# A two-layer decoder trunk on one core: the loop over the layers written out in the code, and the last residual update of a layer interleaved with the split for the next layer's first products

## The chip, the cores and the metric

The kernel runs on one core of one Trainium2 chip. The metric is the device time of one execution in microseconds (us). An execution holds the whole inference step, both layers and all stored states.

## What is computed

The reference is a trunk of two equal layers over 336 tokens (8 running sequences of 8 new tokens, 16 meta tokens, a prompt of 256). In short, with `L` the layer:

```python
for l in range(DEPTH):                                   # DEPTH = 2
    f = swiglu(rmsnorm(x, ln_ffn1_pre[l]), ffn1_w_in[l], ffn1_w_out[l])
    x = x + 0.5 * rmsnorm(f, ln_ffn1_post[l])
    m, s, c, p = mixer(rmsnorm(x, ln_mix_pre[l]), ssm[l], conv[l], pool[l], ...)
    x = x + rmsnorm(m, ln_mix_post[l])
    f = swiglu(rmsnorm(x, ln_ffn2_pre[l]), ffn2_w_in[l], ffn2_w_out[l])
    x = x + 0.5 * rmsnorm(f, ln_ffn2_post[l])
```

The mixer projects `x`, runs a causal convolution of width 4 over 24 tiles of 128 channels, a chunked state-space scan (SSD) over 32 heads, a pooling branch with windows of 2 to 16 tokens, and merges both through sigmoid gates. Everything is float32.

## The kernel before

**Layout.** Activations stand channel-major: `x` is 8 tiles (KD) of 128 channels by 336 tokens. A product with float32 weights is made of three matmuls per 128x128 weight tile. Both operands are split into a high part and the remainder: `gb += whi*ahi + whi*alo + wlo*ahi`. Weights come in units of 8 tiles (512 KB). SyncE loads a unit into one of four slots of `wraw`, ScalarE (ACT) makes `whi` (L430), GpSimd (POOL) makes `wlo` (L355), TensorE (PE) uses both.

**Activations.** For the norm ahead of a product ACT makes `ahi` of each `x` tile and its square (`split_x`, L452, L455), GpSimd adds the squares (L377, L381), and VectorE (DVE) makes `alo` (`split_tile`, L691). The products run on the unnormalised split. Their results are multiplied by the inverse root mean square `rpre` (L681), which arrives later.

**Joins.** I call a join the stretch in which `x` is updated and split for the next products. There are three kinds per layer: after the first feed-forward block (into the mixer), after the mixer (into the second feed-forward block), and between the layers. `update_x` does for each tile `t_a = fo*gain*rms` (L699), `x += t_a` (L701) and a drain (L704). At the first two joins it is called with `nxt`, so that the split of tile `s - 2` stands between the updates. At the join of the layers it is called without. The splits stand at the head of the next pass of the loop over `L`. PE takes the split tiles in `first_units` (L1065 to L1069), four units side by side, so that it can start at the first split tile.

**Mixer.** After its join come 8 convolution tiles (B and C of the scan) and the first of 16 x tiles, as straight code in the body of the layer loop. `conv` multiplies by the first tap (L744) and adds three more (L747), each with a drain ahead. Then come 16 SSD steps. Twelve stand in a hardware loop over `g` with four steps in its body, and the last four are written out behind it. A step on DVE makes, in the order of the code: the convolution of tile t+1, chained states (L787, L792), the masked product (L768), `t_a` (L810, L812, L814, L817), the new states (L825, L826) and the split `blo` (L830). The two operands of L814 and L817 and the weight units of the step hang on the other engines.

Of the kernel before, what the change touches and what calls it, by code (L numbers as in the profile page):

```python
# [23 lines left out]
D_MODEL, D_FF, D_INNER, DEPTH = 1024, 2816, 2048, 2  # L24
# [5 lines left out]
KD, KF, KI = D_MODEL // P, D_FF // P, D_INNER // P  # L30
# [90 lines left out]
def slot_of(phase, n):  # L121

    return (U0[phase] + n) % RING
# [25 lines left out]
def build(nc, x_in, wts, par_in, con_in, own_dram, cst_in, pst_in, ssm_in, y_out, ssm_out, conv_out, pool_out):  # L149
    with ExitStack() as ctx:  # L150
# [177 lines left out]
        @block.sync  # L328
        def _(sp_):
            def unit(u, slot):  # L330
                sp_.wait_ge(w_rawfree, u + 1)
                sp_.dma_start(wraw[:, slot, :], wts[u, :, :]).then_inc(w_landed[slot], 16)

            def units(L, u0, u1):
                with sp_.Fori(u0 // RING, u1 // RING) as i:
                    for s in range(RING):
                        unit(L * UNITS + RING * i + s, s)

            with sp_.Fori(0, DEPTH) as L:
                units(L, 0, U0["f1o"])  # L340
                sp_.wait_ge(s_hfree, L + 1)
                sp_.dma_start(cst[:, :, :], cst_in[L, :, :, :]).then_inc(s_hist, 16)
                units(L, U0["f1o"], UNITS)
            for s in range(AHEAD):
                sp_.wait_ge(w_rawfree, DEPTH * UNITS + s + 1)
                sp_.dma_start(wraw[:, s, :], wts[s, :, :]).then_inc(w_landed[s], 16)

        @block.gpsimd
        def _(pool):  # L350
            pool.sem_inc(w_rawfree, RING)

            def lo(u, s):
                pool.wait_ge(w_hi, u + 1)
                pool.tensor_tensor(wlo[:, s, :], wraw[:, s, :], whi[:, s, :].bitcast(F32), ALU.subtract).then_inc(w_lo, 1)  # L355
                pool.wait_ge(w_lo, u + 1)
                pool.sem_inc(w_rawfree, 1)

            def ahead(L, u):
                lo(L * UNITS + u + AHEAD, (u + AHEAD) % RING)  # L360

            def run(L, u0, u1):

                n = (u1 - u0) // RING
                with pool.Fori(0, n) as i:
                    for s in range(RING):
                        lo(L * UNITS + u0 + AHEAD + RING * i + s, (u0 + AHEAD + s) % RING)
                for u in range(u0 + n * RING, u1):
                    ahead(L, u)

            def sum_x(L, u, n, s0):

                ahead(L, u)
                for k in range(1, KD):
                    pool.wait_ge(sq_done, L * N_SQ + s0 + k + 1)
                    if k == 1:
                        pool.tensor_tensor(acc[:, :], sq[:, 0, :], sq[:, 1, :], ALU.add).then_inc(x_sum, 1)  # L377
                        ahead(L, u + 1)
                    else:
                        pool.wait_ge(x_sum, L * N_XSUM + n * (KD - 1) + k - 1)  # L380
                        pool.tensor_tensor(acc[:, :], acc[:, :], sq[:, k % RING, :], ALU.add).then_inc(x_sum, 1)  # L381

            def ssd_step(L, t, q, last):

                u = U0["ssd"] + 2 * t
                if not last:
                    lo(L * UNITS + u + 1 + AHEAD, slot_of("ssd", 2 * q + 1 + AHEAD))
                pool.wait_ge(dec_done, L + 1)
                pool.wait_ge(st_landed, 16 * (L * KI + t) + 16)
                pool.wait_ge(so_free, 16 * (L * KI + t) + 16)  # L390
                ds_ = dec[:, 2 * DK:].rearrange("p (b h) -> p b h", b=SEQS)[:, :, bass.ds(2 * t, 2)]
                pool.tensor_tensor(so[:, 0:SEQS * P].rearrange("p (b h d) -> p b h d", b=SEQS, h=2),
                                   st[:, :].rearrange("p (b h d) -> p b h d", b=SEQS, h=2), rep(ds_, HEAD_DIM, 3), ALU.mult).then_inc(st_dec, 1)
                lo(L * UNITS + U0["ssd"] + z_at(t, last) + AHEAD, slot_of("ssd", z_at(q + 2, last) + AHEAD))

            for s in range(AHEAD):
                lo(s, s)
            pool.wait_ge(s_con, 32)
            pool.tensor_copy(maskr[:, :], own_in[:, 0:2 * P])
            pool.tensor_copy(identr[:, :], cc(C_ID))  # L400
            pool.tensor_copy(halfr[:, :], own_in[0:HEAD_DIM, 2 * P:4 * P]).then_inc(consts, 1)
            with pool.Fori(0, DEPTH) as L:
                sum_x(L, 0, 0, 0)
                run(L, 2, U0["dt"])
                sum_x(L, U0["dt"], 1, S_X1)
                run(L, U0["dt"] + 2, U0["ssd"] + 1)
                with pool.Fori(0, N_GROUPS - 1) as g:
                    for j in range(TILES_PER_GROUP):
                        ssd_step(L, TILES_PER_GROUP * g + j, j % 2, False)
                for j in range(TILES_PER_GROUP):  # L410
                    ssd_step(L, KI - TILES_PER_GROUP + j, j % 2, j == TILES_PER_GROUP - 1)
                run(L, U0["mix"], U0["f2i"])
                sum_x(L, U0["f2i"], 2, S_X2)
                run(L, U0["f2i"] + 2, UNITS)
# [3 lines left out]
        def _(act):  # L418
# [133 lines left out]
            act.dma_start(con[:, :], con_in).then_inc(s_con, 16)  # L552
            act.dma_start(own_in, own_dram).then_inc(s_con, 16)
            act.wait_ge(s_eps, 1)
            with act.Fori(0, DEPTH) as L:
                split_x(L, G_F1A, 0, 0, "f1i")
                root(L, ST_F1A)
                ffn_in(L, "f1i", V_F1)
# [96 lines left out]
        def _(dve):  # L655
# [32 lines left out]
            def split_tile(L, k, gain, h0):  # L688

                dve.wait_ge(hi_done, L * N_HI + h0 + k + 1)  # L690
                dve.scalar_tensor_tensor(alo[:, k, :], x[:, k, :], pcol(L, gain + k), ahi[:, k, :].bitcast(F32),  # L691
                                         ALU.mult, ALU.subtract).then_inc(a_done, 1)

            def update_x(L, gain, nxt=None):

                lag = 2
                for s in range(KD + (lag if nxt else 1)):
                    if s < KD:
                        dve.scalar_tensor_tensor(t_a[:, s % RING, :], fo[:, s, :], pcol(L, gain + s), kb[0][:, 0:T], ALU.mult, ALU.mult)  # L699
                    if 1 <= s <= KD:  # L700
                        dve.tensor_tensor(x[:, s - 1, :], x[:, s - 1, :], t_a[:, (s - 1) % RING, :], ALU.add).then_inc(val_in, 1)  # L701
                    if nxt and s >= lag:
                        split_tile(L, s - lag, *nxt)
                    dve.drain()  # L704

            def ffn_in(L, ph_, h0, gt0):
# [124 lines left out]
                                         ALU.mult, ALU.subtract).then_inc(b_done, 1)  # L831
                dve.drain()  # L832

            with dve.Fori(0, DEPTH) as L:

                for k in range(KD):
                    split_tile(L, k, G_F1A, 0)
                inverse(L, ST_F1A, rpre)
                ffn_in(L, "f1i", H_F1, 0)
                out_tiles(L, "f1o", S_F1)  # L840
# [155 lines left out]
                ffn_in(L, "f2i", H_F2, KF + KI + 2 * KD)  # L996
                out_tiles(L, "f2o", S_F2)
                inverse(L, ST_F2B)
                update_x(L, G_F2B)

        @block.tensor
        def _(pe):
# [161 lines left out]
                    pe.wait_ge(y_read, kt + 1)  # L1165
                    x_token_major(L, t + 1, 1 - q)

            with pe.Fori(0, DEPTH) as L:
                ffn(L, "f1", 0, 0, 0, ST_F1A, ST_F1B)

                first_units(L, "dt", KD, 1, ST_MA)
# [230 lines left out]
```

## Time and profile before

| what | before |
|---|---|
| time, median of 3 runs | 2289.95 us (2285.34 to 2296.04) |
| profiled execution: span from first to last instruction | 2279.0 us |
| profiled execution: own time | not recorded beside its span; the median of the runs is 10.95 us above the span |
| PE busy | 2087.2 us, 92% |
| DVE busy | 1095.6 us, 48% |
| ACT busy | 937.1 us, 41% |
| POOL busy | 1248.3 us, 55% |
| chain that ended last | PE 64%, DVE 17%, DVEq 10%, issue 5% |

### The profile page before, as it was taken

Reading aid. Unit: us, or ns where it says so; the run is one execution under the profiler, and the core shown is the slowest. Engines: PE = TensorE matmul, PEld = TensorE weight load, DVE = VectorE, ACT = ScalarE, POOL = GpSimd, SP = SyncE. Lnnn points to the kernel's source line nnn. Section 1 sums busy time; section 2 is a strip of 40 time slices with the busy share of each in tenths; the row PEclk is TensorE's granted clock in tenths of the full one; section 3 lists DMA queues with packets and bytes.
Section 4 is the critical chain, followed back from the end, with each engine's and each line's share of the span. In section 5 each row is a group of like instructions: output and inputs, shape, how many; then the busy total and the mean of one; then the engine's idle time right before and its main releaser. Section 6 shows DMA issues by size and latency. Waiting matters only on the chain.

```text
span 2279.0 us, 40931 instructions
## 1 busy us (share of the span) xinstructions
PE 2087.2 (92%) x13546; PEld 2026.9 (89%) x13546; DVE 1095.6 (48%) x2040; ACT 937.1 (41%) x1357; POOL 1248.3 (55%) x555
## 2 busy tenths in 40 slices
PE   6999878999989998999889998699998999989997
PEld 6999877888889997999879998688888999979997
DVE  3221277888944525221242213778888445252212
ACT  4343344444533434333343333444444334343432
POOL 5666642333356665666656676333333566656675
PEclk9999998999999999999999999889999999999998
DMA  4445422333344443444424453223333444434443
GB/s 172 138 144 157 138 67 84 128 118 121 116 150 139 139 143 97 146 139 148 141 91 141 147 156 115 76 97 115 115 115 128 146 139 142 144 99 141 138 156 108
DMA packets 86338, 292.38 MB, mean 128 GB/s; under 512 B 15728, under 2 KB 15728, under 8 KB 86256
## 3 DMA queue, kind: packets, MB, share of 16 engines
q1 hardware_dynamic: 68544, 249.13, 34.6%
q10 hardware_dynamic: 17712, 42.22, 5.3%
q8 instruction: 44, 0.72, 0.1%
q14 instruction: 38, 0.31, 0.0%
HBM read 269.29 MB, written 22.02 MB: 128 GB/s over the span
## 4 chain that ended last, share of the span: by engine, by line
PE 64%; DVE 17%; DVEq 10%; issue 5%; POOL 1%; ACT 1%; DMA 1%; ACTq 0%; POOLq 0%; SPq 0%
PE gb L1013 20%; PE gb L1017 19%; PE gb L1016 19%; DVE cv L747 6%; DVEq L746 2%; DVE t_a L814 2%; DVEq L704 2%; DVEq L832 1%; POOL wlo L355 1%; DVE alo L691 1%; DVEq L777 1%; DVEq L811 1%; PE gb L1065 1%; DVE t_a L699 1%; DVE t_a L812 1%
## 5 line engine op out<-in xcount | busy, mean ns | idle before, releaser
L355 POOL TENSOR_TENSOR wlo<-wraw,whi 128x1024 fp32r<-128x1024 f32 x474 | 1141.7, 2409 | 952.3 <-ACT whi L430 933.2
L1013 PE MATMUL gb<-ahi,whi 128*128 128x336 f32 x2256 | 750.6, 333 | 23.9 <-POOL wlo L355 14.6
L1017 PE MATMUL gb<-ahi,wlo 128*128 128x336 f32 x2256 | 722.5, 320 | 0.0
L1016 PE MATMUL gb<-alo,whi 128*128 128x336 f32 x2256 | 721.9, 320 | 0.0
L430 ACT ACTIVATE whi<-wraw 128x1024 fp32r<-128x1024 f32 x474 | 494.1, 1050 | 188.9 <-PE gb L1013 116.5
L1013 PEld LDWEIGHTS gb<-ahi,whi 128*128 128x128 f32 x2256 | 433.3, 192 | 36.0 <-POOL wlo L355 27.3
L1016 PEld LDWEIGHTS gb<-alo,whi 128*128 128x128 f32 x2256 | 433.3, 192 | 0.0
L1017 PEld LDWEIGHTS gb<-ahi,wlo 128*128 128x128 f32 x2256 | 430.6, 191 | 0.0
L1013 PE MATMUL gb<-bhi,whi 128*128 128x336 f32 x1248 | 395.4, 317 | 5.0 <-DVE blo L967 5.0
L1016 PE MATMUL gb<-blo,whi 128*128 128x336 f32 x1248 | 393.4, 315 | 0.0
L1017 PE MATMUL gb<-bhi,wlo 128*128 128x336 f32 x1248 | 393.1, 315 | 0.0
L713 DVE TENSOR_TENSOR t_a<-gb,rpre 128x336 f32<-128x336 f32 x176 | 88.6, 507 | 337.9 <-PE gb L1017 336.3
L1013 PEld LDWEIGHTS gb<-bhi,whi 128*128 128x128 f32 x1248 | 234.8, 188 | 5.6 <-issue 5.6
L1016 PEld LDWEIGHTS gb<-blo,whi 128*128 128x128 f32 x1248 | 235.3, 189 | 0.0
L1017 PEld LDWEIGHTS gb<-bhi,wlo 128*128 128x128 f32 x1248 | 235.0, 188 | 0.0
L726 DVE COPY fo<-gb 128x336 f32 x48 | 24.4, 508 | 294.0 <-PE gb L1017 294.0
L747 DVE SCALAR_TENSOR_TENSOR cv<-xp,par,cv 128x360 f32<-128x360 f32 x144 | 147.3, 1023 | 29.5 <-issue 29.5
L474 ACT ACTIVATE bhi<-t_b 128x336 f32 (+1 forms) x88 | 42.7, 485 | 249.8 <-DVE t_b L716 249.8
L1065 PE MATMUL gb<-ahi,whi 128*128 128x336 f32 x192 | 68.3, 356 | 52.2 <-DVE alo L691 49.8
L487 ACT ACTIVATE sq<-fo 128x336 f32 x48 | 23.3, 486 | 224.9 <-DVE fo L726 224.9
L495 ACT ACT_TABLE_LOAD x38 | 48.8, 1283 | 136.4 <-DVE cv L747 135.8
L470 ACT ACTIVATE t_b<-t_a 128x336 f32<-128x336 f32 x88 | 42.7, 486 | 119.7 <-DVE t_a L713 119.7
(166 smaller groups left out, 2316.7 us busy)
## 6 DMA issues: line engine op xcount, KB each, us to landing
wraw<-wts SPq DMA_DIRECT2D x474, 512.0 KB, 3.5
ssm_o<-tail ACTq DMA_DIRECT2D x32, 576.0 KB, 3.7
st<-ssm_in ACTq DMA_DIRECT2D x32, 512.0 KB, 4.4
x<-x_in ACTq DMA_DIRECT2D x2, 672.0 KB, 5.0
y<-x ACTq DMA_DIRECT2D x2, 672.0 KB, 3.0
pool_o<-tail ACTq DMA_DIRECT2D x2, 540.0 KB, 4.9
tail<-pst_in ACTq DMA_DIRECT2D x2, 480.0 KB, 4.3
conv_o<-cso ACTq DMA_DIRECT2D x48, 13.5 KB, 3.4
```

What stands on the lines that cost most here:

```text
L355: pool.tensor_tensor(wlo[:, s, :], wraw[:, s, :], whi[:, s, :].bitcast(F32), ALU.subtract).then_inc(w_lo, 1)
L430: act.activation(whi[:, slot, :], wraw[:, slot, :], ACT.Copy).then_inc(w_hi, 1)
L495: act.activation(seqs(dst[:, 0:SAMPLE], STEPS), seqs(cv[:, 0:CP], CSTRIDE)[:, :, 0:STEPS], ACT.Silu, bias=bias)
L704: dve.drain()
L713: dve.tensor_tensor(t_a[:, r, :], gb[r][:, 0:T], rpre[:, :], ALU.mult).then_inc(g_out, 1)
L746: dve.drain()
L747: ins = dve.scalar_tensor_tensor(cv[:, :], xp[:, k:k + n], pcol(L, G_CW + CONV_K * c + k), cv[:, :], ALU.mult, ALU.add)
L814: dve.scalar_tensor_tensor(t_a[:, 2, :], xs[:, q, :], pcol(L, G_D + t), t_a[:, 1, :], ALU.mult, ALU.add)
L1013: ins = pe.matmul(gb[bank][:, 0:T], whi[:, slot, w], xh, start=first and j == 0, stop=False)
L1016: pe.matmul(gb[bank][:, 0:T], whi[:, slot, w], xl, start=False, stop=False)
L1017: ins = pe.matmul(gb[bank][:, 0:T], wlo[:, slot, w], xh, start=False, stop=last and j == tiles - 1)
L1065: ins = pe.matmul(gb[s][:, 0:T], whi[:, s, w], ahi[:, j, :], start=j == 0, stop=False)
```

## The change

The hardware loop over the layers becomes a loop of the program that writes the code: on all five engines both layers are written out, and `L` is a constant. The inner hardware loops stay. `update_x` gets an argument `ahead`, and at the end of layer 0 it is called with the split for layer 1's first products. The splits at the head of a layer remain for layer 0 alone.

```diff
-            with sp_.Fori(0, DEPTH) as L:
+            for L in range(DEPTH):
...
-            with act.Fori(0, DEPTH) as L:
+            for L in range(DEPTH):
...
-            def update_x(L, gain, nxt=None):
+            def update_x(L, gain, nxt=None, ahead=0):
...
                     if nxt and s >= lag:
-                        split_tile(L, s - lag, *nxt)
+                        split_tile(L + ahead, s - lag, *nxt)
                     dve.drain()
...
-            with dve.Fori(0, DEPTH) as L:
-
-                for k in range(KD):
-                    split_tile(L, k, G_F1A, 0)
+            for L in range(DEPTH):
+
+                if L == 0:
+                    for k in range(KD):
+                        split_tile(L, k, G_F1A, 0)
...
-                update_x(L, G_F2B)
+                update_x(L, G_F2B, (G_F1A, 0) if L + 1 < DEPTH else None, 1)
```

(GpSimd and TensorE get the same line in place of their `Fori` over `L`.)

```order
L699 ISA
L699 SCALAR_TENSOR_TENSOR t_a<-fo,par,kb 128x336
L701 TENSOR_TENSOR x<-x,t_a 128x336
L699 ISA
L699 SCALAR_TENSOR_TENSOR t_a<-fo,par,kb 128x336
L701 TENSOR_TENSOR x<-x,t_a 128x336 x2
L834 REGISTER_ALU
L834 COMPARE_AND_BRANCH
```

The head of the loop's body, to which that branch goes:

```order
L834 ISA
L691 ISA
L691 SCALAR_TENSOR_TENSOR alo<-x,par,ahi 128x336
L690 REGISTER_ALU
L691 ISA
L691 SCALAR_TENSOR_TENSOR alo<-x,par,ahi 128x336
```

The same place in the changed kernel, from the first updates on:

```order
L699 SCALAR_TENSOR_TENSOR t_a<-fo,par,kb 128x336 x2
L701 TENSOR_TENSOR x<-x,t_a 128x336
L699 SCALAR_TENSOR_TENSOR t_a<-fo,par,kb 128x336
L701 TENSOR_TENSOR x<-x,t_a 128x336
L691 SCALAR_TENSOR_TENSOR alo<-x,par,ahi 128x336
L699 SCALAR_TENSOR_TENSOR t_a<-fo,par,kb 128x336
L701 TENSOR_TENSOR x<-x,t_a 128x336
L691 SCALAR_TENSOR_TENSOR alo<-x,par,ahi 128x336
```

The eight splits moved up between the updates, as at the other joins. The branch and all register operations of this place are gone.

**Place two: DVE in a step of the SSD loop**, the middle of `ssd_step`. Before, the registers `L` and `g` both enter the sums:

```order
L805 ISA
L806 TENSOR_TENSOR t_b<-gb,rpre 128x336
L810 TENSOR_TENSOR t_a<-kb,eab 128x336
L812 TENSOR_TENSOR t_a<-kb,t_a 128x336
L814 ISA
L814 SCALAR_TENSOR_TENSOR t_a<-t_b,par,t_a 128x336
L816 ISA
L817 TENSOR_TENSOR t_a<-t_a,t_b 128x336
```

In the changed kernel:

```order
L805 REGISTER_ALU
L806 TENSOR_TENSOR t_b<-gb,rpre 128x336
L810 TENSOR_TENSOR t_a<-kb,eab 128x336
L812 TENSOR_TENSOR t_a<-kb,t_a 128x336
L814 ISA
L814 SCALAR_TENSOR_TENSOR t_a<-t_b,par,t_a 128x336
L816 REGISTER_ALU
L817 TENSOR_TENSOR t_a<-t_a,t_b 128x336
```

Operations and their order are the same. Two groups of register operations became single ones, and the group at L814 is left with `g` alone to reckon with.

**Place three: DVE in a convolution of the straight code ahead of the SSD steps.** Before:

```order
L744 ISA
L744 TENSOR_SCALAR cv<-xp,par 128x360
L747 ISA
L747 SCALAR_TENSOR_TENSOR cv<-xp,par,cv 128x360
L747 ISA
L747 SCALAR_TENSOR_TENSOR cv<-xp,par,cv 128x360
```

In the changed kernel these rows are the tensor operations alone:

```order
L744 TENSOR_SCALAR cv<-xp,par 128x360
L747 SCALAR_TENSOR_TENSOR cv<-xp,par,cv 128x360 x3
```

The register operations of all straight code left the stream. The same holds for the four SSD steps that stand behind the loop over `g`.

## Rows read from the trace of the kernel before

**Rows 1.** The page: span, busy time of the engines, instruction fetches, chain by engine.

```profile
span 2279.0 us, 40931 instructions
PE 2087.2 (92%) x13546; PEld 2026.9 (89%) x13546; DVE 1095.6 (48%) x2040; ACT 937.1 (41%) x1357; POOL 1248.3 (55%) x555
q14 instruction: 38, 0.31, 0.0%
PE 64%; DVE 17%; DVEq 10%; issue 5%; POOL 1%; ACT 1%; DMA 1%; ACTq 0%; POOLq 0%; SPq 0%
```

**Rows 2.** Windows: length, busy PE, PEld, DVE, ACT, POOL, then PEclk, DMA share, GB/s.

```profile
378.00:597.00 219.00, 201.93 (x1397) 184.89 (x1395) 189.67 (x348) 106.66 (x173) 79.94 (x36) 0.97 0.37 122
...
897.00:1043.00 146.00, 144.90 (x938) 144.62 (x938) 44.08 (x83) 58.07 (x81) 93.40 (x40) 1.00 0.45 144
...
1132.00:1166.00 34.00, 18.29 (x109) 17.61 (x108) 18.30 (x26) 14.92 (x24) 13.96 (x10) 0.73 0.11 33
```

**Rows 3.** Timeline of DVE: first update and `rpre` of four joins.

```profile
272.14 0.56 DVE L699 SCALAR_TENSOR_TENSOR t_a<-fo,par,kb 128x336 f32<-128x336 f32 x1 [1.86 <-PE kb L1043]
296.91 0.51 DVE L681 COPY rpre<-kb 128x336 f32<-128x336 f32 x1 [4.94 <-PE kb L1043]
...
870.23 0.56 DVE L699 SCALAR_TENSOR_TENSOR t_a<-fo,par,kb 128x336 f32<-128x336 f32 x1 [1.14 <-PE kb L1043]
895.21 0.51 DVE L681 COPY rpre<-kb 128x336 f32<-128x336 f32 x1 [4.95 <-PE kb L1043]
...
1132.36 0.56 DVE L699 SCALAR_TENSOR_TENSOR t_a<-fo,par,kb 128x336 f32<-128x336 f32 x1 [1.86 <-PE kb L1043]
1165.80 0.51 DVE L681 COPY rpre<-kb 128x336 f32<-128x336 f32 x1 [4.95 <-PE kb L1043]
...
2004.51 0.56 DVE L699 SCALAR_TENSOR_TENSOR t_a<-fo,par,kb 128x336 f32<-128x336 f32 x1 [1.27 <-PE kb L1043]
2029.81 0.51 DVE L681 COPY rpre<-kb 128x336 f32<-128x336 f32 x1 [4.94 <-PE kb L1043]
```

**Rows 4.** Timelines of DVE, PE and ACT at the join of the layers.

```profile
1146.70 1.04 DVE L691 SCALAR_TENSOR_TENSOR alo<-x,par,ahi 128x336 fp32r<-128x336 f32 x2 [3.31 <-issue]
...
1147.50 0.64 PE L1065 MATMUL gb<-ahi,whi 128*128 128x336 f32 x1 [15.29 <-DVE alo L691]
...
1148.18 1.06 ACT L430 ACTIVATE whi<-wraw 128x1024 fp32r<-128x1024 f32 x1 [11.18 <-PE gb L1065]
```

**Rows 5.** Timeline of DVE: L812 in SSD steps 4, 6, 12 and 14.

```profile
447.20 0.51 DVE L812 TENSOR_TENSOR t_a<-kb,t_a 128x336 f32<-128x336 f32 x1
...
482.09 0.51 DVE L812 TENSOR_TENSOR t_a<-kb,t_a 128x336 f32<-128x336 f32 x1
...
590.96 0.51 DVE L812 TENSOR_TENSOR t_a<-kb,t_a 128x336 f32<-128x336 f32 x1
...
624.90 0.51 DVE L812 TENSOR_TENSOR t_a<-kb,t_a 128x336 f32<-128x336 f32 x1
```

**Rows 6.** Chain that ended last: start, us, what; one loop step, one written-out step.

```profile
477.24 0.13 DVEq L747
477.42 0.59 DVE cv L747
478.08 0.13 DVEq L747
...
603.77 0.06 DVEq L747
603.83 0.05 issue
603.88 0.59 DVE cv L747
```

**Rows 7.** Timelines of DVE, ACT and POOL in SSD step 5.

```profile
457.25 2.09 DVE L747 SCALAR_TENSOR_TENSOR cv<-xp,par,cv 128x360 f32<-128x360 f32 x1 [0.24 <-issue]
...
457.03 1.92 POOL L392 TENSOR_TENSOR tail<-st,dec 128x1024 f32<-128x1024 f32 x1 [0.44 <-POOL wlo L355]
```

**Rows 8.** Timeline of DVE in the straight code of the mixer.

```profile
317.07 0.59 DVE L747 SCALAR_TENSOR_TENSOR cv<-xp,par,cv 128x360 f32<-128x360 f32 x1 [0.17 <-issue]
...
317.87 0.26 DVE L872 TENSOR_TENSOR sq<-sq 128x96 f32<-128x96 f32 x1
318.20 0.26 DVE L874 TENSOR_TENSOR sq<-sq 128x96 f32<-128x96 f32 x1
```

More of the change, by code:

```diff
@@ L401, in _ @@
             pool.tensor_copy(halfr[:, :], own_in[0:HEAD_DIM, 2 * P:4 * P]).then_inc(consts, 1)
-            with pool.Fori(0, DEPTH) as L:
+            for L in range(DEPTH):
                 sum_x(L, 0, 0, 0)
@@ L832, in ssd_step @@
                 dve.drain()
-            with dve.Fori(0, DEPTH) as L:
-                for k in range(KD):
-                    split_tile(L, k, G_F1A, 0)
+            for L in range(DEPTH):
+                if L == 0:
+                    for k in range(KD):
+                        split_tile(L, k, G_F1A, 0)
                 inverse(L, ST_F1A, rpre)
@@ L1166, in ssd_step @@
                     x_token_major(L, t + 1, 1 - q)
-            with pe.Fori(0, DEPTH) as L:
+            for L in range(DEPTH):
                 ffn(L, "f1", 0, 0, 0, ST_F1A, ST_F1B)
```

## The prediction

> **What bounds the kernel now.** I read the page first. PE is busy for 92% of the span, but the chain that ended last runs through PE for only 64% of it and through DVE and its sequencer for 27% [rows 1]. So there are stretches in which PE isn't the limit. The windows say which. In the feed-forward stretch from 897 to 1043 us PE is busy for 144.9 of 146 us, so nothing that another engine saves there is worth anything. In the 12-step SSD stretch of layer 0, 378 to 597 us, PE has 201.9 of 219 us and DVE 189.7. At the join of the layers, 1132 to 1166 us, PE has 18.3 of 34 us and a mean clock of 0.73 of full speed [rows 2]. The change acts on the two last kinds of stretch, in two ways that I price apart: the splits that move (one place), and the register `L` that becomes a constant (all places).
>
> **The moved splits.** I measure a join from the start of the first update to the start of the copy into `rpre`. Three joins already interleave: 272.14 to 296.91 is 24.77 us, 870.23 to 895.21 is 24.98 us, 2004.51 to 2029.81 is 25.30 us. The join of the layers takes 1165.80 - 1132.36 = 33.44 us [rows 3]. What it does too much is seen in its parts. The first split starts at 1146.70, behind all updates and 3.31 us of idle time that no engine caused: the branch back to the head of the loop. PE waited 15.29 us for that split. ACT, which had stopped after two tiles because it must make a weight tile whose slot PE frees with its first matmul, waited 11.18 us for PE [rows 4]. After the change the DVE stream at this place is that of the other joins, and so are the streams of ACT, POOL and PE, which already were in that order. The new wait on the way is that a split stands ahead of the next update on DVE and waits for ACT's `ahi`. Behind it in the queue stand the next update and, through it, ACT and PE. The three joins contain this wait, so I need no price for it. The gain is 33.44 - 25.02 (their mean) = 8.4 us, with bounds of 8.1 and 8.7 us from the three. SyncE, which loads weights four units ahead, and POOL, whose next `wlo` comes earlier here, have room: the DMA share in this window is 0.11 [rows 2].
>
> **The constant, in the SSD loop.** The operations don't change, their cover does. A register operation costs only where DVE stands idle for it, right behind a drain. In a loop step the fused group at each L747 stands in the chain with 0.13 us. In the four steps that are written out behind the loop, where only `L` is left in the sum, it takes 0.06 us [rows 6]. These four steps are the experiment I need, since a loop step of the changed kernel has only `g` left. From step 4 to step 6 there are 482.09 - 447.20 = 34.89 us, from step 12 to step 14, which stand at the same places of a group of four, 624.90 - 590.96 = 33.94 us [rows 5]. That is 0.475 us a step. Three groups at L747 explain 3 x 0.07 = 0.21 us of it; the rest I put on other groups like them (L733, L814, L816), on ACT and POOL. There are 24 loop steps in the two layers: 24 x 0.475 = 11.4 us. The bounds are nothing and 24 x 0.6 = 14 us.
>
> **The constant, in straight code.** Here the whole operation goes. At L747 DVE is idle for 0.17 us; between two drained operations without a register, 317.87 + 0.26 to 318.20, for 0.07 us [rows 8]. So 0.10 us is saved at each such place. There are 18 convolutions ahead of the loops (9 a layer) and 8 SSD steps behind them with three such places each, 0.30 us. One of the three lies ahead of a stall behind POOL (next part) and I don't count it: 26 x 0.20 = 5.2 us, between 0 and 8 us. In the updates of the joins each of the 8 tiles has one such place. Half of them I take to be hidden by ACT or POOL: 5 joins x 8 x 0.10 / 2 = 2.0 us, between 0 and 4. For the scalars of dt, the pooling start and the ends of the product stages I add 1.0 us, between 0 and 3.
>
> **Code.** The written-out streams are about twice as long, but each engine still runs the same number of instructions in a straight line, and the inner loops stay as they are. I take it to cost nothing. The cover is that instruction transfers run while the engines work: they are 38 packets of 0.31 MB in one queue [rows 1]. What it costs without cover is a rival below.
>
> **Sum.** 8.4 + 11.4 + 5.2 + 2.0 + 1.0 = 28.0 us. The span of 2279.0 becomes 2251.0 us. The median of the runs lies 10.95 us above the span, so I expect 2289.95 - 28.0 = 2262 us, 1.2% less.
>
> **Rivals.**
>
> *Only the join counts (0.07).* GpSimd stalls DVE: the first L747 of step 5 took 2.09 us where an undisturbed one takes 0.59, and ended with GpSimd's product of 1.92 us that began at 457.03 [rows 6, 7]. What DVE saves ahead of such a stall is lost, unless the GpSimd operation moves with it. If these stalls take all savings of registers, 8.4 us are left: 2281.5 us, within 0.5% of before. Against it: the written-out steps have the same stalls and are shorter all the same [rows 5]. The Trainium skill (SBUF — State Buffer, Who interferes with whom) says that the port pair shared by GpSimd and VectorE is an exclusive lock held for a whole instruction, not a split of bandwidth. By that rule each saving ahead of a stall is worth nothing and each behind it is worth all; the 2.09 us of this case agrees.
>
> *PE becomes the limit of the SSD steps (0.08).* PE is busy for 201.9 of 219 us [rows 2], which leaves 17.1 us for about 12 steps, 1.4 us a step. The 0.475 us fit in that, but PE must sit right: if its idle time is needed elsewhere in the step, half of 11.4 and half of 5.2 are lost and the time is 2270 us. Still faster.
>
> *Slower: the loops miss their code (0.03).* The branch back over a whole layer cost DVE 3.31 us of idle time [rows 4]. If an inner loop now lay so that each of its branches back paid that, the price would be 3.31 us an iteration. From the code, DVE takes 28 inner branches back in a layer (two feed-forward inputs of 10, three output loops of 1, the SSD loop 2, the pooling branch 3), 56 in all. It takes (28.0 + 11.4) / 3.31 = 12 of them on the path to make the kernel slower by 0.5%. The SSD loops have 4 and their bodies are the longest, so they alone would only eat 13 us. Against it: no inner branch back shows such a stall now, and nothing but the place of the bodies changes. The Trainium skill (Runtime: NRT & Kernel Launch, Instruction fetch mechanics) says that code is fetched ahead in a straight line, and that a taken branch to a block that isn't held costs a fetch. It calls full unrolling the way around. The 3.31 us of this case agree. By that page, where a body lies against the blocks decides, and the change moves all of them: that is this rival, and no row here can exclude it.
>
> **How the numbers follow.** Forecast 0.82, with its own range of 2250 to 2272 us; the three rivals 0.07, 0.08, 0.03. The low end of my range is all upper bounds, 8.7 + 14 + 8 + 4 + 3 = 38 us, or 2252 us, with 3 us for the spread of the runs, whose extremes lie 0.3% from their median. The high end takes in the case in which PE limits, the lower halves of the terms of registers, and that spread, up to 2278 us. About 0.5% (11.5 us) is what a measurement of this kernel can tell from no change. Faster by more than that: 0.82 of the forecast, nearly all, with 0.08 of the second rival, 0.90. Within: 0.07. Slower: 0.03.
>
> **What would show it.** In the profile of the changed kernel the join of the layers takes 24 to 25.5 us, PE's longest wait there is below 5 us, and the 3.31 us idle time is gone. SSD steps of the loop have the period of the old written-out ones: 33.9 us from the L812 of step 4 to that of step 6, where it was 34.89. The chain shows DVEq L747 with 0.06 in the loop and not at all in straight code, where the idle time ahead of L747 is 0.07 us. If the join shrank and the steps didn't, the first rival is right. If steps shrank and PE's waits in them went, it is the second. Idle time of some 3 us behind inner branches would be the third. A PE clock that falls at other places than now would move some us either way.

## The result, and the profile of the changed kernel

The changed kernel takes 2253.17 us (median of 4 runs, 2248.9 to 2254.58), beside 2287.64 us for the kernel before (2283.06 to 2296.04). The ratio is 0.9831 with a 95% interval of 0.9805 to 0.9857. The runs made beside the experiments give more: the kernel before has a median of 2290.7 us over 79 of them, and the changed one, its first four included, 2254.1 us over 13. So the change saves 36.6 us, 1.6%. I had forecast 28 us, 1.2%. The direction and most of the places are right, the size is a quarter too small.

The page of the changed kernel, the lines that answer to [rows 1], and the group of L747:

```profile
span 2252.3 us, 39690 instructions
...
PE 2086.7 (93%) x13546; PEld 2028.8 (90%) x13546; DVE 1095.7 (49%) x2040; ACT 931.0 (41%) x1354; POOL 1249.5 (55%) x555
...
q14 instruction: 30, 0.25, 0.0%
...
PE 70%; DVE 16%; DVEq 8%; issue 3%; ACT 1%; POOL 1%; DMA 1%; ACTq 0%; SPq 0%
...
L747 DVE SCALAR_TENSOR_TENSOR cv<-xp,par,cv 128x360 f32<-128x360 f32 x144 | 140.3, 975 | 17.8 <-issue 12.4
```

The work is the same: PE has 2086.7 us as before, DVE 1095.7, and ACT alone is 6 us shorter. L747 had 29.5 us of idle time ahead of it before and has 17.8 now. What went is time between operations: PE now holds 70% of the chain where it held 64%.

The join of the layers, timeline of DVE (start, us, what, idle ahead), against [rows 3, 4]:

```profile
1124.32 1.20 DVE L699 SCALAR_TENSOR_TENSOR t_a<-fo,par,kb 128x336 f32<-128x336 f32 x2 [1.74 <-PE kb L1044]
...
1127.10 0.56 DVE L691 SCALAR_TENSOR_TENSOR alo<-x,par,ahi 128x336 fp32r<-128x336 f32 x1
...
1148.49 0.51 DVE L681 COPY rpre<-kb 128x336 f32<-128x336 f32 x1 [4.95 <-PE kb L1044]
```

The first split starts 2.8 us behind the first update (14.3 us before), and the join takes 1148.49 - 1124.32 = 24.17 us instead of 33.44. PE's waits in this stretch are short, where the longest was 15.29 us:

```profile
PE gb L1066 <- DVE alo L691: 4.1, 2, 3.4
```

Its windows row answers to the third of [rows 2]: a PEclk of 0.81 where it was 0.73.

```profile
1122.50:1150.00 27.50, 21.15 (x115) 19.89 (x116) 17.70 (x29) 13.15 (x23) 15.27 (x11) 0.81 0.12 39
```

Two convolutions on the timeline of DVE, in the straight code and in loop step 6, against [rows 7, 8]:

```profile
315.22 1.93 DVE L747 SCALAR_TENSOR_TENSOR cv<-xp,par,cv 128x360 f32<-128x360 f32 x3
...
471.92 2.14 DVE L747 SCALAR_TENSOR_TENSOR cv<-xp,par,cv 128x360 f32<-128x360 f32 x1 [0.18 <-issue]
474.24 0.59 DVE L747 SCALAR_TENSOR_TENSOR cv<-xp,par,cv 128x360 f32<-128x360 f32 x1 [0.17 <-issue]
```

In straight code the three stand in one row with nothing between them but the drain: (1.93 - 3 x 0.59) / 2 = 0.08 us. In the loop the idle time ahead of each is 0.17 us where it was 0.24. The first of step 6 still stalls behind GpSimd, 2.14 us (2.08 us before). In step 5, where [rows 7] has 2.09 us, it now takes 0.59 us: the stall met another operation. The steps 4 and 6 of layer 0 on the timeline of DVE, against [rows 5]; they are 35.05 us apart:

```profile
443.88 0.51 DVE L812 TENSOR_TENSOR t_a<-kb,t_a 128x336 f32<-128x336 f32 x1
...
478.93 0.51 DVE L812 TENSOR_TENSOR t_a<-kb,t_a 128x336 f32<-128x336 f32 x1
```

The chain through a loop step (start, us, what), against [rows 6]:

```profile
1532.47 0.07 DVEq L747
1532.54 0.05 issue
1532.59 0.59 DVE cv L747
```

All the fused groups of this line, by its own view:

```profile
L747 DVEq FUSED_REGOPS  x72: 57/61/65, 364.8 to 1675.1; - x72
```

They were 144 of 57 to 135 ns. Half are gone, the rest cost 0.06 us.

**Where the time went.** Three profiles of each kernel (first ones, and those of experiments e0, e15, e11, e12), cut at the same DVE instructions, both layers together; mean us, and the difference:

| stretch | before | after | difference | forecast |
|---|---|---|---|---|
| join of the layers | 33.5 | 24.2 | -9.4 | -8.4 |
| mixer's straight part, `rpre` to the first loop convolution | 137.4 | 131.4 | -6.0 | -3.6 |
| SSD, step 0 to 12 | 435.0 | 429.4 | -5.6 | -11.4 |
| SSD, step 12 to the copy into `rpost` | 140.1 | 134.6 | -5.5 | -1.6 |
| `rpost` to the join | 423.7 | 420.7 | -3.0 | -1.0 |
| the four other joins | 100.5 | 99.5 | -1.0 | -2.0 |
| all else | 1015.8 | 1015.4 | -0.4 | 0 |
| span | 2285.9 | 2255.2 | -30.8 | -28.0 |

### The profile page after: what moved, and what is told of

It reads as the page before. It is cut to its first block, busy times and chain, and to the rows that moved or that the text cites. A ratio compares the mean times of both kernels' runs of the same rounds, so it can differ in the third digit from the quotient of the medians.

```text
span 2252.3 us, 39690 instructions
## 1 busy us (share of the span) xinstructions
PE 2086.7 (93%) x13546; PEld 2028.8 (90%) x13546; DVE 1095.7 (49%) x2040; ACT 931.0 (41%) x1354; POOL 1249.5 (55%) x555
## 3 DMA queue, kind: packets, MB, share of 16 engines
q1 hardware_dynamic: 68544, 249.13, 33.5%
## 4 chain that ended last, share of the span: by engine, by line
PE 70%; DVE 16%; DVEq 8%; issue 3%; ACT 1%; POOL 1%; DMA 1%; ACTq 0%; SPq 0%
PE gb L1014 21%; PE gb L1017 20%; PE gb L1018 20%; DVE cv L747 5%; DVEq L746 2%; DVE t_a L814 2%; PE gb L1066 1%; PE gb L1069 1%; PE gb L1070 1%; DVEq L704 1%; DVEq L832 1%; DVEq L811 1%; DVE t_a L699 1%; POOL wlo L355 1%; DVE xp L736 1%
## 5 line engine op out<-in xcount | busy, mean ns | idle before, releaser
L747 DVE SCALAR_TENSOR_TENSOR cv<-xp,par,cv 128x360 f32<-128x360 f32 x144 | 140.3, 975 | 17.8 <-issue 12.4
L1148 PEld LDWEIGHTS kb<-bc,st 128*128 128x128 f32 x512 | 90.3, 194 | 0.0
```

The costliest lines, as they stand in the source:

```text
L747: ins = dve.scalar_tensor_tensor(cv[:, :], xp[:, k:k + n], pcol(L, G_CW + CONV_K * c + k), cv[:, :], ALU.mult, ALU.add)
L1148: pe.matmul(kb[1][:, c], st[:, b * P:(b + 1) * P], bc[:, cg, c], start=True, stop=True)
```

## The experiments

**The scatter.** The sum was made against a span of 2279.0 us and applied to a median 10.95 us higher. So I first looked at what those 10.95 us are, with kernels unaltered.

e0, the kernel before:

> The kernel before, run again against itself, to learn how its span relates to its time and how both scatter. The changed kernel's runs lie 1.8 us above their spans, so the profiled execution of before (span 2279.0) should have taken about 2281 us, below every timed run of before (2283 to 2296). Theory 1 (the sum was right for the profiled execution, and before scatters upwards through stretches of lower TensorE clock): spans of the runs scatter from 2279 to 2294 us, the longer ones with a lower mean clock, ratio 0.998 to 1.002. Theory 2 (the time around the span differs between the two kernels): times lie 5 to 11 us above the spans.

e15, the same again, and e11 and e12, the changed kernel:

> The kernel before, unaltered: a second look at its stages. Theory scatter: a span of 2280 to 2295 us that is longer the lower its granted clock, with the joins between the layers at 33 to 34 us, a clean group of four steps at 72.2 to 72.4 us, and the difference to the first profile (2279.0 us) in steps and units where the clock fell, not in the joins. Rival: the first profile was typical, and this one is 2277 to 2281 us again.

> The changed kernel unaltered, beside the three on the same chip. Theory scatter (this kernel's spans lie within 6 us of each other, and its time is 1.8 us above its span): 2249 to 2256 us, profiled span 2247 to 2254 us, joins 24.2 to 25.4 us, and a clean group of four steps 70.9 to 71.1 us, the step from the eleventh to the twelfth 20.1 us again. Rival: the profiled execution after was itself a fortunate one, and the spread is as wide as before (13 us): then a span over 2257 us is among the runs.

> The changed kernel unaltered. Theory scatter (its eight timed runs so far have a median of 2254.4 us and reach from 2248.9 to 2265.7, longer where the mean granted clock is lower): a median of 2252 to 2258 us, a ratio of 0.983 to 0.986, and 0.9 to 1.1 us more for each 0.001 less of mean clock. Rival: the first comparison was right and the last one disturbed; then the median is under 2252 us and the ratio under 0.983.

e0: 2291.23 us (ratio 1.0008, 0.9994 to 1.0022), profiled span 2288.6. e15: 2290.76 (1.0012, 0.9995 to 1.0028), span 2290.2. e11: 2258.6 (0.9846, 0.9803 to 0.989), span 2263.9, above the 2249 to 2256 us that I expected. e12: 2252.59 (0.9841, 0.9818 to 0.9863), span 2249.3. In every kernel the time lies 1.8 us above the span of the same run (up to 2.9). The first profile of before was simply faster than nearly all other runs, whose spans have a median of 2288.7 us. In e11 the rival expectation came true: one span is 2263.9 us, so the changed kernel's runs reach over 17 us, nearly as wide as before's 18.

The scatter sits in single SSD steps. Windows of step 14 to 15 of layer 0, of before in its first profile, then of before in e15 (two fences); behind them PE's one wait in e15's step, which reads the same in both:

```profile
624.90:641.94 17.04, 12.42 (x82) 11.19 (x82) 8.69 (x18) 2.93 (x6) 6.59 (x3) 0.80 0.37 127
```

```profile
627.24:649.29 22.05, 17.43 (x79) 16.10 (x79) 8.67 (x17) 2.93 (x6) 6.58 (x3) 0.56 0.30 99
```

```profile
PE kb L1126 <- DVE tail L826: 4.6, 1, 4.6
```

The same work and the same wait take 5.0 us more, and what differs is the granted clock: 0.80 against 0.56. It is the mean of the two levels, 1.2 and 2.4 GHz, over the step. It tells which step is slow and not exactly how slow: in e0 this step took 22.06 us at 0.63. The changed kernel does the same in its last step of layer 1. First e11, then e12:

```profile
1740.22:1760.64 20.42, 17.71 (x82) 16.38 (x81) 7.17 (x17) 2.49 (x4) 4.96 (x3) 0.59 0.30 107
```

```profile
1733.88:1750.06 16.18, 13.48 (x85) 12.24 (x84) 7.18 (x18) 2.49 (x4) 4.97 (x3) 0.79 0.37 135
```

There PE waits 2.7 us and the bad case costs 4.2 us. Over the 13 runs of the changed kernel the span is 0.91 us longer for each 0.001 less of mean clock (correlation -0.78). Over 78 runs of before it is 1.04 us (correlation -0.89; one more run, with a recorded clock of 0.905, is left out). The median clock is 0.955 before and 0.965 after.

Next I tried to hold the clock up by giving PE more to do. e6 (before) and e7 (changed kernel):

```
-pe.matmul(kb[1][:, SAMPLE:n0], ztile[:, :], bc[:, cg, SAMPLE:n0], start=True, stop=True)
+for _ in range(5):
+    pe.matmul(kb[1][:, SAMPLE:n0], ztile[:, :], bc[:, cg, SAMPLE:n0], start=True, stop=True)
```

> The kernel before, with the last small matmul of each SSD step (the zero columns of kb1, L1149) issued five times in place of once: the results stay, and PE is busy in part of the 1.4 us in which it waits for the chained states. It is to tell whether the granted clock of TensorE in the SSD steps makes the scatter of before (spans 2281.8 to 2294.8 us at mean clocks of 0.960 to 0.948). Theory 1: with PE idle for less, the clock falls less often, the mean clock is 0.960 or more, the spans scatter by less than 6 us and lie at 2277 to 2283 us. Rival (idle time in a step doesn't matter to the clock, or the added matmuls delay the step): the same or longer times, 2289 us or above.

> The same addition to the changed kernel. Theory 1 (its steps have shorter idle times, so its clock falls less already): it gains less than before does, 0 to 5 us, 2248 to 2253 us. If before and after gain alike, the clock has no part in the difference of the two.

e6: 2294.02 us (1.002, 1.0 to 1.004), clocks from 0.949 to 0.963, over 20 us from the fastest run to the slowest. The filling at this place doesn't hold the clock. e7: 2267.94 us (0.9902, 0.9878 to 0.9926), 14 us over the changed kernel, where I had expected 2248 to 2253 us. The pages give the work that was added: PE is busy for 2117.6 us in e6, 30.4 more than before, and for 2120.7 us in e7, 34.0 more than in the changed kernel. Some 2 us of the one and 14 us of the other arrive in the time. So PE has less slack in the changed kernel, but most of the addition is still covered. It isn't in the loop steps that the slack is gone: from step 0 to 12 e7's profile takes 429.9 us in both layers, the changed kernel 429.4. The written-out step from 13 to 14 went from 15.84 to 16.73 us, and from step 12 to `rpost` e7 takes 141.3 us instead of 134.6, part of which can be scatter.

**Writing out against moving.** e1 writes the loops over the layers out and leaves the splits where they were; e13 repeats it.

```
 for L in range(DEPTH):
-    if L == 0:
-        for k in range(KD):
-            split_tile(L, k, G_F1A, 0)
+    for k in range(KD):
+        split_tile(L, k, G_F1A, 0)
...
-    update_x(L, G_F2B, (G_F1A, 0) if L + 1 < DEPTH else None, 1)
+    update_x(L, G_F2B)
```

> All five engines written out, but the splits for layer 1 stay behind the last update: the move alone is undone. Theory 1 (two parts that add up): the join of the layers keeps its order but loses the branch's 3.3 us of idle time, so it takes 29 to 31 us instead of 33.4 before and 24.2 after; the kernel is 5 to 6 us slower than the changed one, and 20 to 22 us faster than before by the spans (ratio 0.988 to 0.992). Rival (the gain is all in the join): the kernel is within 4 us of before.

> All loops over the layers written out, the splits for the next layer left where they were. Theory A: the moved splits are worth the join alone, 28.38 less 24.17 us: 4 us more than the changed kernel on this chip. Theory B: the later start of the second layer's first units also costs clock behind it, as the two medians so far say: 8 to 10 us more.

e1: 2262.26 us (0.9879, 0.9864 to 0.9894). e13: 2259.87 (0.9867, 0.9845 to 0.989). The median of both is 2262.1 over 11 runs, 28.6 us under before and 8.0 over the changed kernel. PE's waits at the join of e1:

```profile
PE gb L1065 <- DVE alo L691: 9.8, 1, 9.8
```

The join takes 28.4 us in e1 and 28.2 in e13. Of the 9.3 us that it lost in the change, 5.1 came with the writing out, and 4.2 with the moved splits. The prediction named the branch's 3.31 us, but booked all 8.4 us under the moved splits. The branch back and the register operations between updates were more than half of it: with them gone and nothing moved, the first split of e1 starts 9.1 us behind the first update, not 14.3. The 8.0 us lie nearer to e13's theory B (8 to 10 us) than to theory A (4 us), though beside each other on one chip e13 and e12 are 7.3 us apart and their intervals overlap. The other 4 of the 8.0 us lie outside the join. Median clocks are 0.961 and 0.965, and at 0.9 us for 0.001 that is 3.6 us. This is a correlation; no run sets the clock by itself.

**Which engine's constant.** e2: DVE alone written out, with the moved splits; the four others keep their loop over `L`.

```
-            for L in range(DEPTH):
+            with pe.Fori(0, DEPTH) as L:
...(and sp_, pool, act alike)
```

> VectorE alone is written out and has its splits moved; ACT, POOL, PE and SyncE run their hardware loops over the layers as before. Theory 1 (what the constant saves is saved mostly by DVE, whose sequencer stood in the chain): 70% or more of the gain stays, a span near 2260 us; the join of the layers takes 25 to 28 us, since ACT and PE still branch back there. Rival (the chain of an SSD step runs through ACT and POOL, whose stalls set DVE's pace): only the join's 8 us and some 5 us more are left, a span near 2266 us or above, with SSD loop steps still 18.0 us.

e3: the opposite, DVE alone keeps its loop, the splits unmoved.

> The counterpart: ACT, POOL, PE and SyncE written out, VectorE with its hardware loop and its old order. Theory 1: the join of the layers stays at 32 to 33.5 us, SSD loop steps lose 0.1 us or less, the span is 2274 to 2277 us. Rival (ACT and POOL set the pace): SSD steps lose 0.2 us or more, and the span falls below 2270 us.

e2: 2267.21 us (0.9909, 0.989 to 0.9928), 23.5 us under before's 2290.7. e3: 2281.59 (0.9964, 0.9951 to 0.9977), 9.1 us under it. Together 32.6 of 36.6 us. DVE, with the moved splits, carries two thirds of the gain and the four other engines a quarter. Both lie between what the theory and its rival expected: e2's span is 2265.2 us and its join 26.47 us, e3's spans reach from 2279.0 to 2286.3 us and its join takes 32.20 us. In e3, where DVE alone still branches back over the layer, the idle time stands as before:

```profile
DVE alo L691 <- issue: 3.2, 1, 3.2
```

The two profiles also say whose gain a stretch is. The mixer's straight part takes 131.4 us in e2 and 137.0 in e3 (137.4 before): it is DVE's. From `rpost` to the join it is the other way round, 423.4 us in e2 and 420.3 in e3 (423.7 before): those 3 us came with the other engines. So did the longer exit of the SSD loop (below): the step from 11 to 12 takes 18.1 to 18.3 us in e2 and 20.3 in e3.

**The rest of the register operations.** The loop over the SSD's groups still keeps `g` in a register. e4 writes it out on all four engines, e8 on DVE, e9 on ACT and POOL, e10 on PE, e14 on DVE and PE. The edit is the same line each time:

```
-                with dve.Fori(0, N_GROUPS - 1) as g:
+                for g in range(N_GROUPS - 1):
```

> The changed kernel with the loops over the groups of the SSD steps written out as well, on DVE, ACT, POOL and PE: no register is left in the 12 loop steps of a layer. Theory 1 (each register operation behind a drain costs about 0.1 us where no stall covers it): steps of the loop fall by another 0.15 to 0.3 us, the kernel by 4 to 8 us against the changed one (2244 to 2248 us). Rival (the stalls behind GpSimd now set the pace): steps within 0.1 us of the changed kernel. Second rival (longer code costs): slower than the changed kernel, with idle time of some 3 us at new places.

> The changed kernel with the loop over the SSD's groups written out on DVE alone; ACT, POOL and PE keep theirs. All four written out saved 17 to 18 us over the changed kernel (2234.03 us). Theory DVE: the register operations and fused groups ahead of DVE's instructions pace the steps, as the prediction had it for this change; then this run has most of the saving, 2238 to 2243 us, and a clean group of four steps takes 67 to 68.5 us. Rival PE: the stream of PE has the last slack (a kernel with about 0.9 us of added matmuls a step was 15 us slower), so its own register operations cost; then this run saves under 4 us (2249 to 2254 us) and a group stays at 70.3 to 71 us. Rival ACT and POOL: likewise under 4 us.

> The changed kernel with the loop over the SSD's groups written out on ACT and POOL alone. Theory DVE and theory PE: within 3 us of the changed kernel (2250 to 2256 us), a group of four steps at 70.5 to 71.3 us. Theory ACT and POOL (the splits into high and low parts that PE waits for are issued there, behind a register operation each): 2236 to 2245 us, a group at 67.5 to 69 us, and the step from the eleventh to the twelfth goes from 20.1 to about 18.5 us.

> The changed kernel with the loop over the SSD's groups written out on PE alone. Theory PE: the matmuls' addresses in registers hold PE up by some tenths of a microsecond in each step, and PE is what the steps go by: 2236 to 2243 us, a group of four steps at 67.3 to 68.7 us. Theory DVE: under 4 us saved, 2249 to 2254 us. If no one engine alone gives more than 5 us and the three together give 17, the step goes by a chain through several engines and the parts do not add up.

> The changed kernel with the loop over the SSD's groups written out on DVE and PE; ACT and POOL keep theirs. DVE alone gave 2239.14 us, PE alone 2251.79, ACT and POOL alone 2267.9, all four 2234.03. If the parts add up, this is within 2 us of DVE alone (2237 to 2241 us) and the four engines should have been slower than it, which they were not. If the gain goes by the slowest chain through DVE and PE, 2232 to 2238 us and a group of four steps at 67.2 to 68 us.

| kernel | median us | ratio to before | 95% interval |
|---|---|---|---|
| changed kernel, e12 | 2252.59 | 0.9841 | 0.9818 to 0.9863 |
| e4, all four | 2234.03 | 0.976 | 0.9731 to 0.9788 |
| e8, DVE | 2239.14 | 0.9782 | 0.9742 to 0.9822 |
| e9, ACT and POOL | 2267.9 | 0.9896 | 0.9856 to 0.9935 |
| e10, PE | 2251.79 | 0.9835 | 0.9794 to 0.9876 |
| e14, DVE and PE | 2236.39 | 0.9769 | 0.9746 to 0.9792 |

Windows of a group of four steps in layer 1, step 4 to step 8, one kernel a fence: before, the changed kernel, e8, e4, e9, e10. Columns as in [rows 2].

```profile
1579.43:1651.68 72.25, 66.44 (x455) 60.74 (x454) 62.18 (x114) 34.96 (x57) 26.67 (x13) 0.96 0.37 121
```

```profile
1556.22:1627.17 70.95, 65.83 (x463) 60.33 (x462) 62.69 (x115) 35.01 (x57) 26.73 (x13) 0.98 0.36 123
```

```profile
1546.76:1615.17 68.41, 64.57 (x463) 58.97 (x462) 64.30 (x115) 34.97 (x57) 26.96 (x13) 1.00 0.39 128
```

```profile
1547.23:1614.36 67.13, 63.57 (x460) 58.68 (x460) 62.75 (x114) 35.30 (x57) 27.51 (x12) 1.00 0.39 131
```

```profile
1567.88:1642.46 74.58, 67.26 (x460) 61.90 (x460) 64.78 (x115) 35.30 (x57) 27.79 (x12) 0.95 0.35 117
```

```profile
1554.89:1626.58 71.69, 68.41 (x463) 63.16 (x462) 62.01 (x114) 34.98 (x57) 26.69 (x13) 0.93 0.36 122
```

The windows give four steps 72.25, 70.95, 68.41, 67.13, 74.58 and 71.69 us. DVE's loop is what counts: e8 has most of e4's gain, and e10 has none that its interval shows. e4 gained 20 us where I had expected 4 to 8; e8 and e10 came out as theory DVE had it. e14's 2236.39 us, with a group of 68.4 us, lies between its two expectations and doesn't decide whether the parts add up. In e8 and e4 the granted clock is 1.00, so it may be that a DVE that keeps PE supplied is paid twice; no run sets the clock apart. PE's own register operations are hidden. Writing DVE's loop out also takes out its branch back: of the four steps in each window one stands behind it, and DVE idles there for 1.01 us before and 0.82 in the changed kernel, register operations included. No run parts the two.

That ACT and POOL alone cost time was expected by none of the theories: 14 us over the median of the 13 runs, 9 us over e11, which ran beside it. DVE's groups by line say where. The changed kernel, then e9, then e4, in the same windows:

```profile
L747 DVE SCALAR_TENSOR_TENSOR cv<-xp,par,cv 128x360 f32<-128x360 f32 x12 | 13.3, 1111 | 2.1 <-issue 2.1
L740 DVE COPY cso<-xp 128x24 f32<-128x24 f32 x4 | 8.7, 2180 | 0.4
L814 DVE SCALAR_TENSOR_TENSOR t_a<-t_b,par,t_a 128x336 f32<-128x336 f32 x4 | 6.8, 1688 | 0.8 <-issue 0.8
...
L768 DVE TENSOR_TENSOR sq<-sq,fo 128x512 f32<-128x512 f32 x4 | 2.7, 683 | 0.0
...
L769 DVE TENSOR_TENSOR sq<-sq,fo 80x160 f32<-80x160 f32 x4 | 1.3, 313 | 0.0
```

```profile
L747 DVE SCALAR_TENSOR_TENSOR cv<-xp,par,cv 128x360 f32<-128x360 f32 x12 | 9.9, 826 | 2.1 <-issue 2.1
L769 DVE TENSOR_TENSOR sq<-sq,fo 80x160 f32<-80x160 f32 x4 | 7.7, 1931 | 0.0
L740 DVE COPY cso<-xp 128x24 f32<-128x24 f32 x4 | 7.2, 1795 | 0.4
...
L768 DVE TENSOR_TENSOR sq<-sq,fo 128x512 f32<-128x512 f32 x4 | 4.9, 1220 | 0.0
L736 DVE COPY xp<-cst 128x24 f32 x4 | 3.7, 914 | 3.7 <-PE gb L1018 2.9 <-issue 0.8
...
L814 DVE SCALAR_TENSOR_TENSOR t_a<-t_b,par,t_a 128x336 f32<-128x336 f32 x4 | 2.3, 569 | 0.8 <-issue 0.8
```

```profile
L768 DVE TENSOR_TENSOR sq<-sq,fo 128x512 f32<-128x512 f32 x4 | 4.9, 1220 | 0.0
L769 DVE TENSOR_TENSOR sq<-sq,fo 80x160 f32<-80x160 f32 x4 | 3.4, 852 | 0.0
```

POOL does the same work, 27 to 28 us. But it begins at other moments, and its stalls of DVE moved from the end of the output (L814, 1688 to 569 ns) to the products with L (L768, L769). DVE then waits 2.9 us for PE at L736, 0.6 in the changed kernel, and PE's clock is at 0.95. That the stalls moved is shown; that they cost the 9 to 14 us is not. e4 has them at L768 and L769 too, shorter at L769, and it is the fastest. The loss of e9 also has a place: its profile takes 448.7 us from step 0 to 12, 19 more than the changed kernel, and 125.9 from step 12 to `rpost`, 9 less. The Trainium skill (SBUF — State Buffer, Who interferes with whom) calls the port pair of GpSimd and VectorE an exclusive lock held for a whole instruction. The trace agrees: an 80x160 product of L769 takes 1.93 us in the mean here and 0.31 us in the changed kernel.

**Everything written out.** e5 writes out every inner loop of all engines, the feed-forward ones too.

> Every hardware loop written out on all engines, SyncE and the feed-forward stages too: DVE's, ACT's and PE's code grows some fivefold in the feed-forward stages. Theory 1: there PE is busy for all of the time, so nothing is gained beyond the SSD loops; within 3 us of the kernel with the SSD loops written out. Rival (instruction fetches of long straight code hold an engine up): 10 us or more slower than that, with PE idle times in the feed-forward stages that weren't there.

2240.45 us (0.9788, 0.9761 to 0.9814), 6 us more than e4, between the two expectations and with an interval that overlaps e4's. The feed-forward stretches take 945.0 us in both layers, 947.5 in e4: PE bounds them, as the prediction said. What e5's profile loses against e4's, it loses for the most part in irregular SSD steps. Why, I did not settle. e4 has the lowest median here, 2234.03 us, though the intervals of e14, e8 and e5 overlap its own.

## Why the prediction was right and wrong

**In short.** The signs and the places came out, the sizes didn't. Three terms failed. The SSD loop was put at 11.4 us and gave 5.6. The straight code was put at 5.2 + 1.0 us and the same stretches gave 14.5. And nothing was added when a sum made on one profiled execution was carried to the median of the runs, between which the change is 9.7 us larger than between the two first profiles. The first two errors nearly cancel, so that 28.0 us stands near the 30.8 us of the profiles by luck.

**The moved splits and the join.** Right in place and nearly in size: 8.4 forecast, 9.3 measured, with the three signs (24 to 25.5 us, longest wait of PE below 5 us, no 3.31 us of idle time). The cause was split wrongly: 4.2 us belong to the move and 5.1 to the lost branch and register operations (e1, e13). The bounds from the other joins were too narrow. This one takes 24.2 us in all three profiles, a value that no join of before had and that others of the changed kernel have in some executions.

**The constant in the SSD loop.** The step that failed in the sum is "That is 0.475 us a step. ... 24 x 0.475 = 11.4 us". The group of four steps went from 72.25 to 70.95 us, 0.33 a step. From step 0 to step 12 the mean over three profiles is 5.6 us for 24 steps, 0.23 a step. The sign that I gave, 33.9 us from step 4 to step 6, was 34.27 in layer 1 and 35.05 in layer 0. The comparison that I used as an experiment, loop steps against written-out ones, compared more than the register: the written-out steps stand at the end of the SSD with other work beside them. And it was one pair out of several that scatter: the same pair of steps in layer 1 of the same profile takes 34.88 us, against 34.91 in its loop, which would have given 0.02 us a step. In e0 and e15 it takes 33.96 to 34.69 us. The 3 x 0.07 us at L747 were right to the hundredth. What I added for other groups and engines was not. In the four steps of the windows above, DVE's trace holds 95 register operations before (94 fused groups of 8.9 us together) and 95 in the changed kernel (62 fused groups of 4.2 us, 33 single ones of 1.3), and none in e8. So 3.4 us went and the group became 1.3 us shorter; then 5.5 us went, and the branch back with them, and it became 2.5 us shorter. Some 0.4 of what DVE's sequencer saves arrives at the end. Also, the step from 11 to 12, the exit of the loop, now takes 20.1 us in all profiles of the changed kernel (18.3 to 18.7 in those of before, 18.4 in e4's layer 1). POOL is busy for 9.2 us in it and DVE for 18.8, where before they were 7.4 and 16.8, so that another stall of DVE probably fell into it. It gives back some 1.5 us a layer. By e2 and e3 it comes with the writing out of the other engines.

**The constant in straight code.** The step that failed is the count in "26 x 0.20 = 5.2 us" and the 1.0 us for the rest. The straight part of the mixer alone gave 6.0, the last SSD steps 5.5 and the pooling part ahead of the join 3.0, in the means. The single price was right (0.17 us of idle time down to 0.08), but I counted L747 only, in streams in which other drained operations have such a place. For the mixer's part e2 bears this out, where DVE alone gives all of it. The 3.0 us of the pooling part came with the other engines (e3), whose constants the sum had at nothing here. By which of them is open. The 5.5 us hold scatter: that stretch spans 129.0 to 140.8 us in three profiles. The count was also off by itself. The last step of a layer has no convolution, so there are 6 and not 8 behind the loops, and the sum should have read 24 x 0.20 = 4.8 us.

**The updates of the joins.** 2.0 forecast, 1.0 measured for four of them, not to be told from nothing.

**From the span to the median.** The step that failed is "The median of the runs lies 10.95 us above the span, so I expect 2289.95 - 28.0 = 2262 us". Only 1.8 us of them lie around the span. The rest is that the profiled execution was a fast one, with a mean clock of 0.961 where the median is 0.955; by 1.04 us for 0.001 that is some 6 of the 9 us. Profile against first profile the change gave 2279.0 - 2252.3 = 26.7 us, against 28.0 forecast. Median against median of the spans it gave 2288.7 - 2252.3 = 36.4 us. The difference of 9.7 us belongs to no operation that I can name. The clock rose by 0.010 between the medians and by 0.003 between the two profiles, and at 0.9 us for 0.001 that is some 6 us of it. So a term was missing, put at nothing: what the change does to the scatter of the runs. I had it only as a remark, "some us either way". That the clock falls less because PE waits less would explain it, but it is not shown: e6 and e7 changed what PE does between its waits and neither raised the clock.

**Rivals.** *Only the join counts* is refuted: e1 keeps most of the gain without the moved splits. Its mechanism is real, though: the stalls move with POOL, from step 5's L747 to another operation in the changed kernel and from L814 to L768 and L769 in e9, and e9 is slower. *PE becomes the limit* is half true: e7 shows that PE has less slack, but e8 shows that DVE still sets the pace. *The loops miss their code* did not happen. Instruction packets in queue q14 fell from 38 to 30, and no idle time of 3 us stands behind an inner branch. The Trainium skill (Runtime: NRT & Kernel Launch, Instruction fetch mechanics) has a taken branch wait for a fetch when its target isn't held. Here idle times of some 3 us (3.31 before, 3.21 in e3) stand behind DVE's branch over a whole layer alone.

## What to carry to other kernels

Behind a drain of VectorE a group of register operations took 0.06 to 0.13 us here, and PE's own in the SSD loop cost nothing that e10 can show. So loop variables in addresses are first taken out of the engine that drains most and supplies PE: here one more line, DVE's loop over groups, was worth 15 us more (2254.1 less 2239.14). Before summing against a profile, see whether its span plus the constant around it (1.8 us here) is a typical run; if not, the scatter is in the kernel, and the change may move it too. A comparison of two pairs of steps says little before it is made in the other layer and in a second profile. Writing one engine's loop out shifts its instructions against the others; ACT and POOL alone made it slower, all four together had the lowest median.

## What the hardware showed that I had not expected

- One SSD step with the same work and the same wait of PE takes 17.04 or 22.05 us before, and 16.18 or 20.42 in the changed kernel. The granted clock in it is 0.80 or 0.56, and 0.79 or 0.59; in a third profile 22.06 us went with 0.63.
- Five times the zero matmuls on PE changed neither the clock nor its scatter (0.949 to 0.963) in the kernel before.
- The branch back over a layer left DVE idle for 3.31 us and ACT for 2.68. The one over the four steps of the SSD loop left DVE idle for 1.01 us and ACT for 1.50, register operations included.
- At L747 a fused group of register operations takes 0.13 us with two variables in its sum and 0.06 with one; a single register operation takes 0.04 us.
